# Neighbourhood and full attention with the values stationary, the softmax division ahead of the turn, and the turns shared between two PSUM banks

## The reference, cut to what matters

```
def hybrid_layer(x, ...):
    h = rms_norm(x, norm_g)
    qa, ka, va, za, qb, kb, vb, zb, ga, gb = split_cols(einsum('bld,de->ble', h, w_in))
    oa = gqa_attention(qa, ka, va) * silu(za)            # 8 heads of 64, every key: softmax(q k^T) v
    ob = neighbourhood_attention(qb, kb, vb, rpb) * silu(zb)   # 8 heads, a window of keys + bias + meta keys
    ya = einsum('ble,ed->bld', oa, w_o_attn)
    yb = einsum('ble,ed->bld', ob, w_o_na)
    mixed = sigmoid(ga) * ya + sigmoid(gb) * yb
    return x + einsum('bld,de->ble', mixed, w_out)
```

## Time and profile before

| | |
|---|---|
| median of 3 runs | 1154.15 us (1152.8 to 1155.03) |
| the profiled execution, its own time | 1154.66 us |
| its span | 1152.8 us |
| PE, PEld busy | 97%, 95% |
| DVE busy | 71% |
| ACT busy | 54% |
| POOL busy | 22% |
| TensorE clock granted, mean | 0.996 |
| attention loop of layer 0, of layer 1 | about 74 to 204 us, about 302 to 419 us |

### The profile page before, as it was taken

One profiled execution on the slowest core, in us unless ns is written; L12 is line 12 of the kernel. 1 busy time (PEld: TensorE's weight loads), 2 busy tenths in 40 slices (PEclk: granted clock), 3 DMA queues, 4 the chain that ended last, 5 costly groups with the idle time before them and its releaser, 6 DMA issues.

```text
span 1152.8 us, 23113 instructions
## 1 busy us (share of the span) xinstructions
PE 1120.4 (97%) x9124; PEld 1098.1 (95%) x9124; DVE 823.8 (71%) x1842; ACT 619.3 (54%) x1154; POOL 254.9 (22%) x213
## 2 busy tenths in 40 slices
PE   6999999999999999999999999999999999999997
PEld 6999999999999999999999999988999999999997
DVE  6964356779544678787766799677856887777666
ACT  6555545564655547544444554464455564444555
POOL 1056553200665714000000007400770000000000
PEclk9999999999999999999999999999999999999999
DMA  6454332354533434555445654324543545554551
GB/s 244 157 183 147 111 119 93 135 183 138 186 133 119 153 119 169 211 199 202 161 176 182 214 184 147 110 74 167 186 162 139 196 166 189 190 179 157 195 209 37
DMA packets 38778, 185.04 MB, mean 161 GB/s; under 512 B 12552, under 2 KB 14984, under 8 KB 20240
## 3 DMA queue, kind: packets, MB, share of 16 engines
q1 hardware_dynamic: 38672, 183.57, 45.4%
HBM read 182.49 MB, written 1.06 MB: 159 GB/s over the span
## 4 chain that ended last, share of the span: by engine, by line
PE 82%; DVE 13%; ACT 2%; issue 2%; DMA 1%; POOL 0%; DVEq 0%; SPq 0%; ACTq 0%
PE line L2216 51%; PE result L2216 18%; DVE w_lo L1377 4%; PE line L2529 2%; PE turn L2373 1%; PE result L2407 1%; PE score L2350 1%; PE score L2548 1%; PE stat L2407 1%; PE score L2354 1%; PE score L2216 1%; DMA h<-in_tokens 1%; ACT w_hi L882 1%; DVE prod L1699 1%; PE line L2226 0%
## 5 line engine op out<-in xcount | busy, mean ns | idle before, releaser
L864 POOL TENSOR_TENSOR w_lo<-raw,w_hi 128x512 fp32r<-128x512 f32 x168 | 224.5, 1368 | 542.3 <-ACT w_hi L882 542.2
L1377 DVE TENSOR_TENSOR w_lo<-raw,w_hi 128x512 fp32r<-128x512 f32 (+2 forms) x546 | 338.4, 664 | 3.3 <-ACT w_hi L917 2.0
L2216 PE MATMUL line<-x_hi,w_hi 128*128 128x256 f32 (+1 forms) x1048 | 310.2, 296 | 15.9 <-DVE x_lo L1429 9.0
L2216 PE MATMUL line<-x_hi,w_lo 128*128 128x256 f32 (+1 forms) x1048 | 299.4, 286 | 0.0
L2216 PE MATMUL line<-x_lo,w_hi 128*128 128x256 f32 (+1 forms) x1048 | 299.0, 285 | 0.0
L882 ACT ACTIVATE w_hi<-raw 128x1024 fp32r<-128x1024 f32 (+2 forms) x178 | 179.7, 1009 | 91.8 <-PE line L2216 36.7
L2216 PEld LDWEIGHTS line<-x_hi,w_hi 128*128 128x128 f32 x1048 | 199.5, 190 | 23.2 <-issue 16.6
L2216 PEld LDWEIGHTS line<-x_lo,w_hi 128*128 128x128 f32 x1048 | 199.4, 190 | 1.4 <-issue 0.5
L2216 PEld LDWEIGHTS line<-x_hi,w_lo 128*128 128x128 f32 x1048 | 199.9, 191 | 0.0
L2216 PE MATMUL line<-y_hi,w_hi 128*128 128x256 f32 (+1 forms) x656 | 192.6, 294 | 1.0 <-DVE y_lo L1437 0.3
L2216 PE MATMUL line<-y_hi,w_lo 128*128 128x256 f32 (+1 forms) x656 | 185.4, 283 | 0.0
(11 more groups left out here) (393 smaller groups left out, 2294.0 us busy)
## 6 DMA issues: line engine op xcount, KB each, us to landing
raw<-in_weights SPq DMA_DIRECT2D x144, 1024.0 KB, 4.8
raw<-in_weights SPq DMA_DIRECT2D x32, 704.0 KB, 4.0
rel_raw<-in_rpb SPq DMA_DIRECT2D x64, 24.0 KB, 4.8
h<-in_tokens SPq DMA_DIRECT2D x2, 544.0 KB, 6.4
raw<-in_weights SPq DMA_DIRECT2D x2, 512.0 KB, 6.0
rbias<-bias_by_distance SPq DMA_DIRECT2D x8, 128.0 KB, 4.5
out<-wide SPq DMA_DIRECT2D x4, 256.0 KB, 2.9
consts<-in_consts SPq DMA_DIRECT2D x1, 960.0 KB, 7.1
```

The costliest lines, as they stand in the source:

```text
L864: pool.tensor_tensor(w_lo[:, u % CUT, at], raw[:, u % RAW, at], w_hi[:, u % CUT, at].bitcast(F32), ALU.subtract).then_inc(lo_pool, 1)
L1377: dve.tensor_tensor(w_lo[:, u % CUT, at], raw[:, u % RAW, at], w_hi[:, u % CUT, at].bitcast(F32), ALU.subtract).then_inc(lo_cut, 1)
L2216: ins = pe.matmul(bank[:, 0:n], stay, move[:, first + k, 0:n], start=(k, m) == (0, 0), stop=(k, m) == (depth - 1, 2))
```

## The change

1. `exps` of an A or B job no longer writes `probs` in SBUF but leaves the exponentials in the job's score bank. A new step `evenly(job)` on DVE, at the head of DVE's step t+1, takes the reciprocal of the row sum (128 x 1) and multiplies the bank into `probs`. `turn` waits for it (`evened`), and so does the next use of that score bank. `normal_of` loses its division, `head_out` goes.
2. `values` has V stationary (64 columns, for the shared tile 128) and the turned probabilities moving (128 columns). The result has the head's features on the partitions, straight in `pair_bank(job)`, which is result bank 0 or 1 by pair c. `pair_out` (32 transposes in the program) goes.
3. The stat bank, no longer used for A and B values, takes every other turn (`IN_STAT`); a turn waits only for the copy of the turn before it in its own bank (`TURN_FREE`). Jobs right behind `("Am", 0)` and `("Bm",)` stay in the turn bank.
4. `TAIL` is 2: `result_of`, `round_y` and `rest_of_y` come one step earlier, and the 32 fillers are spread over one step less. The blank steps are now 7, 11, 15, 19, 23 in layer 0 and 7, 11 in layer 1; step 27 (layer 0) and 15 (layer 1) have a filler, and all later fillers come one step earlier relative to the jobs.

The diff, cut:

```
-TAIL = 3
+TAIL = 2
...
+def turns_in_stat(i):
+    held = {JOBS[i].index(j) + k for j in (("Am", 0), ("Bm",)) if j in JOBS[i] for k in range(1, 4)}
+    n, jobs = 0, set()
+    for at, job in enumerate(JOBS[i]):
+        if n and at not in held:
+            jobs.add(job)
+        n = (job not in jobs)
+    return jobs
...
+TURN_FREE = {(_i, _j): max([TURN[(f"layer{_i}", *_k)] + 1 for _k in JOBS[_i][:JOBS[_i].index(_j)]
+                            if (_k in IN_STAT[_i]) == (_j in IN_STAT[_i])], default=JOB[_i]) ...}
...
-    single_bank = [stat_bank, result_bank[1]]
-    pair_bank = result_bank[0]
+    def pair_bank(job):
+        return result_bank[(PAIRS * (job[0] == "B") + job[1]) % 2]
...
             def exps(job, n):
-                if place >= 2:
+                if place >= 2 and len(job) != 4:
                     act.wait_ge(turn_done, ...)
...
-                act.activation(probs[0:m, place % 2, first:first + keys], score_bank[s % 2][0:m, 0:keys],
+                powers = score_bank[s % 2] if len(job) == 4 else probs[:, place % 2, first:]
+                act.activation(powers[0:m, 0:keys], score_bank[s % 2][0:m, 0:keys],
...
+            def evenly(job, n):
+                if len(job) != 4:
+                    return
+                dve.wait_ge(exped, n + 1)
...
+                if place >= 2:
+                    dve.wait_ge(turn_done, TURN_OF_JOB[LAST_OF_PLACE[place - 2]] + 1)
...
+                link(dve.reciprocal(share[:, pair % 2, half:half + 1], total[:, pair % 2, half:half + 1]))
+                dve.tensor_scalar(own, powers, share[:, pair % 2, half:half + 1], None, ALU.mult).then_inc(evened, 1)
...
             def normal_of(job, n):
-                dve.wait_ge(valued, n + 1)
-                link(dve.reciprocal(share[:, pair % 2, 0:2], total[:, pair % 2, 0:2]))
-                dve.tensor_tensor(head_out[:, pair % 2]..., single_bank[pair % 2]..., ALU.mult).then_inc(normal, 1)
...
             def result_of(job, n):
-                    dve.wait_ge(paired, PAIRED[(i, job)] + 1)
+                    dve.wait_ge(valued, n + 1)
...
             for t in range(J + TAIL + 2):
+                if 1 <= t <= J:
+                    evenly(jobs[t - 1], JOB[i] + t - 1)
                 if t < J:
                     maxes(jobs[t], JOB[i] + t)
...
             def turn(job, n):
                 if len(job) == 4:
-                    pe.wait_ge(exped, n + 1)
+                    pe.wait_ge(evened, 2 * PAIRED[(i, job)] + job[2] + 1)
...
-                r, place = TURN[(name, *job)], PLACE[(i, job)] % 2
-                if r:
-                    pe.wait_ge(turned_most, r)
+                place, into = PLACE[(i, job)] % 2, stat_bank if job in IN_STAT[i] else turn_bank
+                if TURN_FREE[(i, job)]:
+                    pe.wait_ge(turned_most, TURN_FREE[(i, job)])
...
-                        cols = slice(0, P) if b == both else own
-                        ins = pe.matmul(single_bank[pair % 2][:, cols], tn[:, b * P:(b + 1) * P], v[:, kt, cols],
-                                        start=(half, b) == (0, 0), stop=b == both)
+                        rows = slice(0, P) if b == both else own
+                        ins = pe.matmul(pair_bank(job)[rows, t * P:(t + 1) * P], v[:, kt, rows], tn[:, b * P:(b + 1) * P],
+                                        start=b == half, stop=b == both)
...
-            def pair_out(job):
...
-                pe.wait_ge(normal, pair + 1)
-                pe.transpose(pair_bank[:, t * P:(t + 1) * P], head_out[:, pair % 2], ident).then_inc(paired, 1)
```

More of the change, by code:

```diff
@@ L390 @@
         SCORE_READ[(_l, *_j)] = ("maxed" if _j[0] == "Bm" else "exped", JOB[_i] + _n + 1)
+        if len(_j) == 4:
+            SCORE_READ[(_l, *_j)] = ("evened", 2 * PAIRED[(_i, _j)] + _j[2] + 1)
 for _f in range(2):
@@ L441 @@
         if _k[0] == "layer1":
-            _last[4] = ("exped", JOB[1])
+            _last[4] = ("evened", 4 * KT)
         if _k[0] in ("layer1", "ffn0"):
@@ L476, in rel_unit @@
     return UNIT[(f"layer{i}", *FILLERS[min(f + 3, len(FILLERS) - 1)])] + RAW
+def turns_in_stat(i):
[6 more added lines that the diff above has]
+    return jobs
+IN_STAT = [turns_in_stat(_i) for _i in range(DEPTH)]
+TURN_FREE = {(_i, _j): max([TURN[(f"layer{_i}", *_k)] + 1 for _k in JOBS[_i][:JOBS[_i].index(_j)]
+                            if (_k in IN_STAT[_i]) == (_j in IN_STAT[_i])], default=JOB[_i])
+             for _i in range(DEPTH) for _j in JOBS[_i]}
 METAS = sum(len(_j) != 4 for _i in range(DEPTH) for _j in JOBS[_i])
-def pairs_to(i, n):
-    return sum(JOB[k] + JOBS[k].index(j) <= JOB[i] + n for k, j in PAIRED if j[2] == 1)
 def metas_to(i, n):
@@ L596, in hybrid_blocks_kernel @@
     turn_done, turned_most = sem("turn_done"), sem("turned_most")
-    normal, paired = sem("normal"), sem("paired")
+    evened = sem("evened")
     valued, even_scores = sem("valued"), sem("even_scores")
@@ L1019, in exps @@
                 if len(job) == 4 and half == 0 and PAIRED[(i, job)] >= 2:
-                    act.wait_ge(normal, PAIRED[(i, job)] - 1)
+                    act.wait_ge(evened, 2 * (PAIRED[(i, job)] - 1))
                 first, keys = half * (P + HD), KEYS_B
@@ L1036, in turned_of @@
                     act.wait_ge(valued, n - 1)
+                from_ = stat_bank if job in IN_STAT[i] else turn_bank
                 if job[0] == "Bm":
-                    out_, in_ = turned[0:META, n % 2, 0:P], turn_bank[0:META, 0:P]
+                    out_, in_ = turned[0:META, n % 2, 0:P], from_[0:META, 0:P]
                 else:
@@ L1598, in maxes @@
                 dve.tensor_reduce(top[0:m, n % 2, 0:1], bank[0:m, 0:TOK], AX.X, ALU.max, negate=True).then_inc(maxed, 1)
+            def evenly(job, n):
+                if len(job) != 4:
+                    return
+                dve.wait_ge(exped, n + 1)
+                pair, half, place = PAIRED[(i, job)], job[2], PLACE[(i, job)]
+                if place >= 2:
+                    dve.wait_ge(turn_done, TURN_OF_JOB[LAST_OF_PLACE[place - 2]] + 1)
+                first, keys = (half * (P + HD), KEYS_B) if job[0] == "B" else (half * SECOND, TOK)
+                own, powers = probs[:, place % 2, first:first + keys], score_bank[SCORE[(name, *job)] % 2][:, 0:keys]
+                link(dve.reciprocal(share[:, pair % 2, half:half + 1], total[:, pair % 2, half:half + 1]))
+                dve.tensor_scalar(own, powers, share[:, pair % 2, half:half + 1], None, ALU.mult).then_inc(evened, 1)
             def shares(job, n):
@@ L1692, in layer @@
                 if TAIL <= t < J + TAIL:
-                    result_of(jobs[t - TAIL])
+                    result_of(jobs[t - TAIL], JOB[i] + t - TAIL)
                 if t >= TAIL + 2:
@@ L2368, in turn @@
                         at = slice(hd * META, (hd + 1) * META)
-                        ins = pe.transpose(turn_bank[0:META, at], probs[0:META, place, at], ident[0:META, 0:META])
+                        ins = pe.transpose(into[0:META, at], probs[0:META, place, at], ident[0:META, 0:META])
                 else:
@@ L2372, in turn @@
                     for b, (first, _) in enumerate(tiles_of(job)):
-                        ins = pe.transpose(turn_bank[:, b * P:b * P + m], probs[0:m, place, first:first + P],
+                        ins = pe.transpose(into[:, b * P:b * P + m], probs[0:m, place, first:first + P],
                                            ident[0:m, 0:m])
@@ L2442, in layer @@
                     values(jobs[t - 2], JOB[i] + t - 2)
-                if t >= TAIL:
-                    pair_out(jobs[t - TAIL])
             two_lines([(name, "yb", 0), (name, "yb", 1)], W, y_of[name], PAIRS, PAIRS, (0, PAIRS),
```

43 lines of the change are left out of this document (13 added, 30 removed).

## The result

The kernel before takes 1154.01 us (median of 4 runs, 1152.8 to 1155.03), the changed one 1171.12 us (median of 4, 1169.04 to 1172.73). The ratio is 1.0144, 95% interval 1.0128 to 1.0159: 17.1 us slower, where the forecast was 2.6 us faster.

The account below looks back on a forecast made before the run. PE, busy 97% of the span, was taken to bound the kernel. PE's work -2.5 us and gaps -0.1 gave -2.6: 1152.1 profiled, 1151.6 us as median (-0.22%), range 1148.3 to 1157.0.

Parts of the forecast that it names:

- `pair_out`, -3.8 us: PE in the attention loops: 32 transposes of `head_out` go, at 0.12 us each, -3.8 us.
- Values at 0.11 a record, +1.3 us: PE's values records, all with 128 moving columns, cost 0.11 us each: half 0 +1.6 us, half 1 -0.3.
- Rival 3: Values: V's weight load isn't hidden; 0.14 a record gives 1157.4 us, fully added about 1161; chance 0.07.
- DVE's work, +19 us, hidden; the multiply short: `evenly` adds 35.5 us, the pair's division saves 16.2; idle DVE time absorbs it, with multiplies of 0.436 and 0.340.
- The gaps, -0.1 us: PE's waits in the two attention loops: gains and losses nearly cancel, summing to -0.1 us.
- Step 2: Both layers: `evenly` stands behind the stretched gate product, so the turn waits 0.35 us; +0.7 for both.
- Blank step 7: The turn waits for `evened` behind the gate product: +0.3 us in layer 1, +0.2 in layer 0.
- The `ya` places, +1.6: First `ya` line and `ya` 4: values wait for ACT's copy behind two roundings, +0.8 us per layer, +1.6 with both places.
- The other gains: Blank steps 11, 15, 19 and 11: -0.6 us; 23: -0.7; removed 27 and 15: -0.8; loop ends: -0.8.
- Rival 2: Steps with `ya`: DVE becomes what PE waits for, +2.5 us in all, 1156.7; chance 0.16.
- the stretched bias: Within rival 2: a bias stretched to 2.2 us on DVE adds 1.5 us at each first `ya`.
- Outside the loops: Stages outside the two attention loops are PE-bound and stay unchanged.

Follow-up runs that it names:

- e8: The kernel before, its 32 transposes of `head_out` written as plain fp32 matmuls with the identity, 128 columns loaded: 1159.06 us, 1.0040 of before.
- e1: The changed kernel with every values matmul loading all 128 columns of V (output isn't the reference's): 1156.46 us, 1.0015 of before.
- e5: The changed kernel with whole 128-column loads from V zero-padded in SBUF, computing the reference: 1156.40 us, 1.0016 of before.
- e12: e5 without the division; ACT writes exponentials to SBUF and the turn waits for them: 1149.26 us, 0.9954 of before.
- e6: The kernel before, with the transposes of `head_out` loading 64 of 128 columns: 1153.64 us, 0.9994 of before.
- e9: As e8, but the 32 plain matmuls load 64 columns instead of 128: 1165.19 us, 1.0095 of before.

## Why the prediction was wrong

- **`pair_out`, -3.8 us:** right. Its records are gone, and doubling them in e8 lengthened the loops by 3.3 us.
- **Values at 0.11 a record, +1.3 us:** the step that failed. Its sentence was that a 64-column load hides behind even 64 moving columns, since six such records take 0.49. I read a mean over a run of equal loads and took it for the price of the load; the price is at the run's edges, which the mean hides, and at the next matmul behind it, which I did not count as touched. The term is right to 0.01 us for whole loads (0.45, 0.67, 0.22, 0.45 in e1) and missed 64 x 0.33 = 21 us for the narrow ones. 14.7 us of it reached the time. The kernel before had the warning twice. The first stands in the chain 1.4 us behind the six records that I had read (104.54). The second run of six is followed by scores that take 0.66 us, where they take 0.46 behind whole loads (at 115.29):

```profile
105.97 0.49 PE stat L2391 x6
106.47 0.66 PE score L2350 x2
```

The second is in its weight loads by form (74 to 430 us):

```profile
L2407 PEld LDWEIGHTS stat<-va,turned 128*128 128x128 f32 x80 | 10.2, 191 | 0.0
...
L2391 PEld LDWEIGHTS stat<-turned,va 128*64 128x64 f32 x12 | 0.8, 137 | 0.2 <-issue 0.2
```

80 whole loads have no idle time, 12 narrow ones have 0.2 us, 0.17 of it in front of the run that stands behind whole 128x128 loads (at 105.90). With 0.20 us at the record behind the narrow ones, 64 jobs come to 13 us from the first warning alone.
- **Rival 3** (V's load not hidden, 1157.4 to 1161, chance 0.07) had the place and the sign. It put the price on each record, where it lies on the passage, and so came to +5.8 or about +10 us where the chain has +21. The Trainium skill ("TensorE: Matmul & The Clock Gate", Part 3, The mechanism) lets a load overlap a matmul only where the row group differs. The runs do not agree as it stands: e1's loads all use the same rows and hide (0.45 for four records). Its +10 us was nearer to the result than my 0, but for another reason than the one that the runs show.
- **DVE's work, +19 us, hidden; the multiply short:** right in the changed kernel but for the waits in the next item, with the multiply 15% and 18% dearer than its nearest rows. In the changed kernel, DVE by form (74 to 434 us):

```profile
L1626 DVE TENSOR_SCALAR probs<-score,share 128x272 f32<-128x272 f32 x32 | 16.0, 501 | 1.1
L1626 DVE TENSOR_SCALAR probs<-score,share 128x176 f32<-128x176 f32 x32 | 12.8, 401 | 1.1
L1625 DVE RECIPROCAL share<-total 128x1 f32<-128x1 f32 x64 | 9.9, 154 | 1.1 <-ACT score L1038 1.1
```
  38.7 us instead of 35.5. All 64 multiplies lie between 400 and 503 ns: none is stretched beside POOL.
- **The gaps, -0.1 us:** wrong by 3.9 in the loops of e5, 4.8 by the medians. Step 2 was right: +0.7, and PE waits 0.36 and 0.31 us for the division there (e1_whole). Blank step 7 was +0.5 for both layers: PE waits 1.10 us in layer 0 and 1.25 in layer 1. I had taken the gate product's length from before (0.81) as its own; it depends on where in a subtraction of POOL the product starts, as above, and in layer 1 it went from 0.81 to 1.45 us. The `ya` places, +1.6: 2.5 us for ACT's copy, the right mechanism, undersized. The other gains are real: without the division the loops are 5.0 us shorter than before (e12), which is the forecast's -2.5 of PE's own work and 2.5 from the gaps, where the forecast's gaps without the waits for the division (0.7 and 0.5) come to -1.3. The division in front of the turn eats this gain. Rival 2 (the DVE is waited for) was thus present too, at waits in steps 2 and 7 rather than in every `ya` step; its own sum counts the stretched bias once (1.5) though it names it for both layers.
- **Outside the loops:** nothing changed, as said: 98.4 us before and 98.3 after between the loops, 733.6 and 733.4 behind them (from the first `yb` line of layer 1 to the end).

Without the narrow loads the result is 1156.4: inside the range, but slower than before where faster was forecast, so the mechanism of the gaps had failed even there. Two terms were wrong, and the large one was the one with rows in the trace that contradicted it.

## What to carry to other kernels

Where short fp32 matmuls follow each other, count the passages between loads of different width, not the columns: in this kernel a job with narrow stationary operands between wide ones cost 0.33 us more, about 0.13 on the way in and 0.20 on the way out, and padding with zeros to the full width gave it back for some SBUF (loops of 247.4 us in e5 as in e1). Look for it in the idle time of the weight loads put down to "issue"; the busy share of PE hides it. A term that rests on a mean over a run needs the run's first and last record looked at apart; and a wait removed from a chain (turns, by the early division) counts only once the next one in line (ACT's copy) has been read.

## What the runs showed of the hardware that I had not expected

- Loads of equal shape, 128 or 64 columns, hide behind 128 moving columns (0.11 us a record in both cases: the 0.58 for four narrow ones less 0.13 for the passage, and e1's 0.45 for four whole ones); a change of width to or from the narrow load of a plain fp32 matmul exposes the load, with 0.17 us of idle time in front of it, also where the wide load in front is a transpose's (the turn). The score records behind it take 0.20 us more for two.
- The same change of width in a transpose costs nothing (e6: idle 0.1 us for 32 loads; e9: 6.9 us in the three groups for 64 passages).
- A gate product (`scalar_tensor_tensor`, both inputs in SBUF) that starts while POOL subtracts `w_lo` ends 0.28 to 0.30 us after the end of that subtraction, whenever it started: 153 of the 159 such products in the attention loops of the 14 profiles. The other six started in the last 0.06 us of a subtraction and took their usual 0.42 to 0.43; the longest took 1.54. The multiply from PSUM is not held: 0.50 us at 105.65, inside a subtraction of POOL (e1).
- ACT writes exponentials in place into PSUM no slower than into SBUF: 0.462 us for 128x272 in the changed kernel against 0.488 before (means of 32), 0.380 against 0.408 for 128x176.
